# A two-stream transformer kernel on one core: GpSimd's additions moved to VectorE, and head tiles handled in pairs

## What is computed

```python
for layer in range(2):                       # first stack, stream x
    h = rms_norm(x, ln_mix_pre[layer])
    m = even_mixer(h) if layer == 0 else odd_mixer(h)
    x = x + rms_norm(m, ln_mix_post[layer])
    h = rms_norm(x, ln_ffn_pre[layer])
    x = x + rms_norm(swiglu(h, gate, up, down), ln_ffn_post[layer])
for i in range(2):                           # second stack, streams h and hc
    h, hc = half_ffn(h), half_ffn(hc)
    y, yc = diff_attention(h, hc) if i == 0 else gqa_attention(h, hc)
    h = gated_residual(h, y); h = half_ffn(h)
    if i == 0: hc = gated_residual(hc, yc); hc = half_ffn(hc)
return h
```

## Time and profile before

| | |
|---|---|
| median of three runs | 2799.68 us |
| the profiled execution's own time | 2801.2 us |
| its span, first to last instruction | 2799.5 us |
| TensorE busy (matmul) | 2588.8 us |
| VectorE busy | 1694.4 us |
| ScalarE busy | 1251.0 us |
| GpSimd busy | 132.2 us |
| mean granted TensorE clock | 0.959 |

### The profile page before, as it was taken

How to read it: one execution, slowest core, us unless ns; L and a number is a source line. 1 busy time by engine, 2 the same in 40 slices (tenths; PEclk the granted TensorE clock), 3 DMA queues, 4 the chain that set the end, 5 groups by cost and what they waited for, 6 DMA issues and landing times.

```text
span 2799.5 us, 48887 instructions
## 1 busy us (share of the span) xinstructions
PE 2588.8 (92%) x20706; PEld 2461.9 (88%) x20706; DVE 1694.4 (61%) x2807; ACT 1251.0 (45%) x1698; POOL 132.2 (5%) x174
## 2 busy tenths in 40 slices
PE   6799998999998999999898999999999998987998
PEld 5699988888888899999797989999999998966998
DVE  5665564456666556466666757676566566555654
ACT  4533342344444344454444544454454454334443
POOL 0000000000012000000020000020000010000000
PEclk9899998899999999999899999999999999988999
DMA  6556655523445665544342334554545544444453
GB/s 231 196 187 248 242 181 193 211 104 108 166 163 199 222 247 185 192 153 155 103 144 83 121 124 168 179 174 165 182 168 181 177 166 144 165 147 170 151 178 124
DMA packets 68616, 475.80 MB, mean 170 GB/s; under 512 B 7984, under 2 KB 8496, under 8 KB 14768
## 3 DMA queue, kind: packets, MB, share of 16 engines
q1 hardware_dynamic: 66240, 468.74, 47.3%
q10 hardware_dynamic: 2160, 3.93, 0.5%
HBM read 471.60 MB, written 1.05 MB: 169 GB/s over the span
## 4 chain that ended last, share of the span: by engine, by line
PE 71%; DVE 11%; issue 7%; ACT 6%; DMA 4%; POOL 1%; ACTq 0%; DVEq 0%; POOLq 0%
PE bank L249 61%; ACT whi L208 4%; DVE wlo L228 2%; DMA raw<-w_main 2%; PE bank L994 2%; DVE wlo L215 1%; DMA raw<-w_down 1%; PE bank L876 1%; PE bank L814 1%; PE bank L1323 1%; PE bank L736 1%; DVE ARX L656 1%; DVE HNC_lo L670 1%; PE bank L760 1%; PE bank L864 1%
## 5 line engine op out<-in xcount | busy, mean ns | idle before, releaser
L249 PE MATMUL bank<-HNX_hi,whi 128*128 128x256 f32 x2968 | 866.4, 293 | 54.8 <-DVE wlo L228 30.9
L249 PE MATMUL bank<-HNX_hi,wlo 128*128 128x256 f32 x2968 | 851.8, 288 | 0.0
L208 ACT ACTIVATE whi<-raw 128x2048 fp32r<-128x2048 f32 (+1 forms) x378 | 705.6, 1867 | 306.2 <-PE bank L249 138.8
L249 PE MATMUL bank<-HNX_lo,whi 128*128 128x256 f32 x2968 | 838.5, 288 | 0.0
L215 DVE TENSOR_TENSOR wlo<-raw,whi 128x1024 fp32r<-128x1024 f32 (+1 forms) x378 | 454.3, 1202 | 605.5 <-ACT whi L208 604.8
L249 PEld LDWEIGHTS bank<-HNX_hi,whi 128*128 128x128 f32 x2968 | 585.9, 197 | 75.1 <-issue 46.1
L249 PEld LDWEIGHTS bank<-HNX_hi,wlo 128*128 128x128 f32 x2968 | 585.7, 197 | 0.0
L249 PEld LDWEIGHTS bank<-HNX_lo,whi 128*128 128x128 f32 x2968 | 577.8, 197 | 0.5
L228 DVE TENSOR_TENSOR wlo<-raw,whi 128x1024 fp32r<-128x1024 f32 (+1 forms) x378 | 453.1, 1199 | 0.0
L249 PE MATMUL bank<-HNC_hi,whi 128*128 128x256 f32 x1344 | 395.9, 295 | 20.2 <-DVE tmpc L428 9.5
L249 PE MATMUL bank<-HNC_lo,whi 128*128 128x256 f32 x1344 | 386.6, 288 | 0.0
(11 more groups left out here) (320 smaller groups left out, 3134.8 us busy)
## 6 DMA issues: line engine op xcount, KB each, us to landing
raw<-w_main SPq DMA_DIRECT2D x270, 1024.0 KB, 4.8
raw<-w_ada SPq DMA_DIRECT2D x72, 1024.0 KB, 4.8
raw<-w_down SPq DMA_DIRECT2D x72, 1024.0 KB, 4.9
raw<-w_down SPq DMA_DIRECT2D x36, 768.0 KB, 4.2
raw<-w_cmp SPq DMA_DIRECT2D x4, 1024.0 KB, 4.7
HX<-x_in SPq DMA_DIRECT2D x2, 512.0 KB, 6.2
HC<-ctx_in ACTq DMA_DIRECT2D x1, 1024.0 KB, 7.3
out<-HX SPq DMA_DIRECT2D x4, 256.0 KB, 2.1
```

The source lines that it names most:

```text
L208: NS.activation(WHI[q % HIS][:, 0:size], RAW[m % SLOTS][:, 0:size], ACT.Copy).then_inc(sems["w_hi"], 1)
L249: return NT.matmul(dst, (WHI[ordinal[n] % HIS], WLO[n % SLOTS])[w][:, k * 2 * P + col:k * 2 * P + col + P], x[xp][:, kx, :], start=start, ...
```

## The change

GpSimd keeps only two small tasks at the start (a memset and a mask). The other edits go with it: the residual additions and lane c's sums of squares become VectorE instructions, lane c's steps in a norm are set 6.0 instead of 2.5 apart, a job of lane c is put into the program at the first step of lane x after a further block was taken, and `turn` and `tile_norm` work on pairs of head tiles: 21 rotations (20 pairs and one single) instead of 41, and 16 pairs instead of 32 tiles.

```diff
+            def catch_up():
+
+                if "c" in jobs and len(taken) > behind[0]:
+                    settle(C)
@@ after
                 last, jobs[S.tag] = jobs.get(S.tag), job
+                behind[0] = len(taken)
@@ put_out
-                    if on(adder, sq, ss0 if k > 1 else None):
-                        E.tensor_tensor(S.YY, S.YY, S.SQ[k % len(S.SQ)], ADD).then_inc(ss.sem, 1)
-                    if on(adder, gg, gs0 if k > 1 else None):
-                        E.tensor_tensor(S.GG, S.GG, S.DIAG, ADD).then_inc(gs.sem, 1)
+                    if on(dve, sq, ss0 if k > 1 else None):
+                        NV.tensor_tensor(S.YY, S.YY, S.SQ[k % len(S.SQ)], ADD).then_inc(ss.sem, 1)
+                    if on(dve, gg, gs0 if k > 1 else None):
+                        NV.tensor_tensor(S.GG, S.GG, S.DIAG, ADD).then_inc(gs.sem, 1)
@@ norm, add_back
-                    if on(pool, sc):
-                        NG.tensor_tensor(S.H[:, k, :], S.H[:, k, :], S.TMP[k % 2][:, 0:T], ADD).then_inc(re.sem, 1)
+                    if on(dve, sc):
+                        NV.tensor_tensor(S.H[:, k, :], S.H[:, k, :], S.TMP[k % 2][:, 0:T], ADD).then_inc(re.sem, 1)
@@ norm
                     if t == "c" and j % 2 == 0:
-                        yield ("L", 2.5)
+                        yield ("L", 6.0)
@@ turn
+                n = tiles.shape[1]
+                swapped, kept = (x[:, 0:n * T].rearrange("p (a b) -> p a b", a=n) for x in (bank, TMPX[j % 2]))
-                    NT.matmul(bank[:, 0:T], rot, tile, start=True, stop=True).then_inc(turned.sem, 1)
+                    NT.matmul(swapped, rot, tiles, start=True, stop=True).then_inc(turned.sem, 1)
-                    NV.tensor_tensor(TMPX[j % 2][:, 0:T], bank[:, 0:T], sin, MUL).then_inc(part.sem, 1)
+                    NV.tensor_tensor(kept, swapped, sin.unsqueeze(1).to_broadcast([P, n, T]), MUL).then_inc(part.sem, 1)
@@ tile_norm
-                    if j % 2:
-                        yield ("L", 0.6)
+                    yield ("L", 0.8)
-                        for c in range(2):
-                            mm = NT.matmul(sums[:, 2 * j + c:2 * j + c + 1], b[:, c * P:(c + 1) * P], ones[:, 0:1], start=True, stop=True)
+                        for c in range(4):
+                            mm = NT.matmul(sums[:, 4 * j + c:4 * j + c + 1], b[:, c * P:(c + 1) * P], ones[:, 0:1], start=True, stop=True)
@@ tile_norm, diagonal
-                        for c in range(2):
-                            op = NV.tensor_scalar(b[:, c * P:(c + 1) * P], ident, buf[:, 2 * j + c:2 * j + c + 1], None, MUL)
+                        NV.tensor_tensor(b.rearrange("p (c q) -> p c q", c=4), ident.unsqueeze(1).to_broadcast([P, 4, P]),
+                                         buf[:, 4 * j:4 * j + 4].unsqueeze(2).to_broadcast([P, 4, P]), MUL).then_inc(diag.sem, 1)
@@ tile_norm, the loop over pairs
-                        if j % 2 == 0:
-                            yield ("L", 0.8)
+                        yield ("L", 1.0)
                         spread(j, diag)
-                        if len(S.SQ) > 1 and j + 1 < n:
+                        if len(wide) > 1 and j + 1 < n:
                             diag = diagonal(j + 1)
-                        scale_tile(j)
+                        scale_pair(j)
@@ fill and pace, first line of each
+                catch_up()
```

107 lines of the change are left out of this document (58 added, 49 removed).

## The result

Four runs of the changed kernel gave a median of 2737.6 us (2732.9 to 2739.2), four of the kernel before on the same chip 2799.5. The ratio is 0.9776 with a 95% interval from 0.9756 to 0.9796: 63 us less, between 57 and 68. The forecast was 2772 us with a range from 2748 to 2799. The sign and the order of events were right; the size was not.

What follows compares the result with a forecast made beforehand. TensorE, busy 2588.8 of 2799.5 us, was taken as the bound; terms -15 - 5 - 12 - 13 + 4 + 6 + 8 = -27 us from 2801.2 gave 2774, set to 2772 us for extra clock; range 2748 to 2799.

Steps and rivals of the forecast that it cites:

- The pairs: Head norms and rotations: waits for spreads and squares fall by 15 of 19.3 us, the grouped attention by 5.
- The -5 for the grouped attention: Grouped attention, where nothing covers head norm and rotations: VectorE's work there falls from 23 to 17.3 us, -5 us.
- 6.0: Lane c's norms: less crowding on VectorE gains 13 us; lost filling costs 6 in the first norm, 8 in the third.
- The fourth and fifth norm: Lane c's norms under lane x's dense blocks: 6.0 gains 5 us for both together.
- The first norm: Lane c's first norm: 6.0 takes two filler blocks from lane x's first norm with an addition, +6 us (+2 to +12).
- The third: Lane c's third norm, in lane x's differential attention: dense work returns some three iterations later, +8 us (+3 to +14).
- the rival of starvation: Rival: lane c's longer norms take the filling from lane x, costs 50 + 4 against gains of 45, 2810 us; chance 0.12.
- Lane c's sums and jobs: Ends of lane c's stages: the 7.7 us wait near 860 us and three smaller ends go, -12 us (-5 to -15).
- The additions of lane x's norms: Ten norms of lane x with additions on VectorE: 1.46 us a tile, slower pipeline filling, +4 us (0 to +6).
- VectorE's balance: VectorE's busy time: +70.9 us of additions, -33.8 without GpSimd, -20.9 by pairs, +16 us in all; still 61 to 62% busy.
- Gaps that only move: Rival: late cuts and waits turn up elsewhere, half of the gains against costs of 18, 2797 us; chance 0.20.
- The port rule in full: Rival: GpSimd holds up more than durations show, nearly all gaps behind `wlo` go, 15 us more, 2754 us; chance 0.13.

Runs made afterwards that it cites:

- The five single values: Changed kernel with one norm of lane c at 2.5, first to fifth in turn: +11, +7, -4, +6, +10 us against the changed kernel.
- the catch-up alone: Kernel before with only lane c's jobs put in at lane x's first step after a further block was taken: 0.9947, -15 us.
- narrow pairs: Kernel before with rotations and head norms in pairs, but rotation and spread matmuls issued as two of 256 columns: 0.9898, median 2769.3 us.

## Why the prediction was wrong

The step that failed is the sum's view of TensorE: it added up waits, and put what TensorE's own instructions would save at about 4 us of clock (2 at the gap of 860 us, and 2 from 2774 to 2772). Measured are 36.6 us of idle time and 27.0 us of busy time. Most of the latter, some 21 us, is the clock: 227 fewer dense matmuls at 1.2 GHz. The prediction had named the stretches at the lower clock that follow gaps, so the mechanism was there and its size was not. By terms:

**The pairs (sum -20, measured -34).** The term counted waits alone, and took 15 of 19.3 us. The waits went beyond that (26.7 us): the rotations' own 10.0 us and some of lane x's head norms' were not in the 19.3. What has no term is TensorE's busy time: the matmuls of 41 rotations, of 32 spreads and of the sums of squares of 32 tiles stood at 72.6 us in its groups, and coming by twos took 12.2 us off, by an estimate like the one above some 7 through the pairing itself and some 5 through the clock. The prediction had just said that time can be won "in the 211 us in which TensorE stands still, and in the stretches at the lower clock". The odd mixer, with 15 rotations and 4 head norms, has no term at all and gave 7.2 us: in its groups of small matmuls 4.0 us of waits and 3.2 of busy time. The -5 for the grouped attention came out in size (-4.6 in its stage).

**6.0 (sum -13 + 6 + 8 = +1; measured -9 alone, -15 within the whole).** Mis-sized in four places. The clock: by the estimates above, dense matmuls at full clock make 10 us alone, as much as the whole gain, and 13 of the 15 within the whole, and for them the sum had no number of its own. The fourth and fifth norm, taken at 5 together, showed 5.8 and 5.4 us in their stages: the working of the second norm (two tiles in each half-block don't fit) holds for each norm beside dense blocks, and it should have been used three times. The first norm had the wrong sign: the filler lost there was worth even 12.6 us of waits, but 13.3 us of waits behind the blocks' cuts and a sum went with it, of which the forecast had taken back only 5.5 (11.5 less 6); and the filler was taken to be lost for good, while it is put off to a place where it is worth more; why, was not taken apart. The third cost 4 where 8 was forecast. Of the loss in the grouped attention the rival of starvation had spoken, and it is there: lane c comes later, and this stage is 8.0 us longer with 6.0 alone. That it took back most of stage 8's gain was not in my sum. The five single values make 11 + 7 - 4 + 6 + 10 = 30 us against 15 for all at once: they all shift lane c's place, and so don't add.

**Lane c's sums and jobs (sum -12 for both; measured 0 and -15).** The gap at 860 us went as forecast, by the catch-up: it is gone with the catch-up alone and back without it. But a job that comes one late isn't the matter of one place with three small ends: the catch-up is called at each half-block and gave something in five stages, most in the odd mixer, that the forecast doesn't name.

**The additions of lane x's norms (+4; measured 0).** The pipeline was right to 0.01 us a tile (1.45). The filling was probably paid where other work stood; that is argued, not shown.

**VectorE's balance (+16; measured -1.0).** Additions 70.2 us as forecast (70.9), rotations -9.3 (-9.0). Without GpSimd the groups fell by 42.1 us instead of 33.8, 33.5 in the four that were priced; the difference is line 352 of lane c (619 to 425 ns, 5.4 us) and the cuts (3.2 us), which I had not listed. The rest is argued only: the moved additions stand directly behind others and overlap them by 0.08 us, as in the rows of the norm above (1657.37 + 0.41 against 1657.70), 168 x 0.08 = 13 us of busy time that isn't counted twice. Nothing hung on this.

**The rivals.** Gaps that only move: not so, the idle time fell by 36.6 us. The port rule in full: refuted by the run with the additions alone. Nor does "about half" of GpSimd's instruction hold for all that it held up: line 350 of lane c lost 431 of some 900 ns, lines 668 and 670 on average 177 and 200 of 732. The Trainium skill, "SBUF — State Buffer", section "SBUF: two separate sides", says why an instruction of VectorE is held up by GpSimd, and the trace agrees (853 to 420 ns); it is no guide to the time of this kernel, where those instructions were not what TensorE waited for. Starvation: its mechanism is present at a size of 8 us (6.0 alone, in the grouped attention) and 4 us (third norm), and was outweighed. The long wait for lane c ahead of the grouped attention, which the prediction had named as a sign of being wrong, is there: TensorE's line 828 waits 4.9 us for lane c's keys (`KC`, line 776). But with all norms at 2.5 the same line waits 5.0 us for a rotation, so it costs nothing by itself.

**What held.** VectorE stays at 62%; no gap near 860 and 910; the wide diagonal at 0.69 us; the second norm's 8 us (7 measured). The clock came back far more than priced, from 0.959 to 0.967 on average. The time lost by it (one minus the granted clock, times the length) went from 114 to 90 us; part of this is in every term above.

## What to carry to other kernels

Where the busiest engine is busy for nine tenths, price what an edit does to its busy time as well as its waits. A closed gap gives back more than the gap: here 36.6 us less of idle time came with 27.0 us less of busy time, most of it, by estimate, matmuls that now ran at 2.4 GHz. And read the clock beside every mean duration before you call a difference the instruction's own. When a program lane gives way to another, its work isn't lost but put off; ask what stands where it lands. And an interference that is plain in one engine's durations is worth an experiment before it is worth a change: 42 us of it weighed nothing.

## What the runs showed of the hardware

A float32 spread of 256 columns took TensorE 0.59 us of busy time when it stood alone at a granted clock of 1.00 (1389.01 us) and 1.22 us at 0.50 behind a wait of 2.36 us (1397.78 us, both in the kernel before); two that followed each other at 1.00 took 1.02 us (1374.46 us, narrow pairs), and as one of 512 columns 1.04 us on average (5.2 us for 5). The means of the groups, 0.80 us alone (8.0 us for 10, lane c) against 0.52 in twos (5.2 us for 10), mix the two levels of the clock. Dense matmuls of 256 columns followed each other at 0.12 us at 2.4 GHz and at 0.21 at 1.2. VectorE's TensorTensor with both operands broadcast, 128x512, took 0.69 us, no more than with plain ones. The scaling of 512 columns out of PSUM took 0.74 us against 2 x 0.48.
